# Behind its last product TensorE makes 315 more on consumed buffers, with shifted and strided operands

## The reference

```python
def second_block(x, c, ...):
    c_act = jax.nn.silu(c)
    for l in range(DEPTH_2):
        ...
        x = x + g1 * token_mix(h, w_in[l], w_fourier[l], w_ret[l], w_out[l])
        h = rmsnorm_2(x, norm2_g[l]) * (1.0 + sc2) + sh2
        x = x + g2 * conv_ffn(h, ffn_up[l], conv_w[l], conv_b[l], ffn_down[l])
    return rmsnorm_2(x, final_g)
```

## Time and profile before

| | |
|---|---|
| device time, median of 2 runs | 2907.27 us |
| the two runs | 2906.2 and 2908.34 us |
| span of the profiled execution, first to last instruction | 2902.9 us |
| device time of the profiled execution itself | not listed apart from the two runs |
| TensorE products, weight loads | 19658 each |
| busy: PE, PEld, DVE, ACT, POOL | 99%, 83%, 54%, 38%, 55% |
| mean granted TensorE clock | 0.999 |

### The profile page before, as it was taken

How to read it: one execution, slowest core, us unless ns; L and a number is a source line. 1 busy time by engine, 2 the same in 40 slices (tenths; PEclk the granted TensorE clock), 3 DMA queues, 4 the chain that set the end, 5 groups by cost and what they waited for, 6 DMA issues and landing times.

```text
span 2902.9 us, 49417 instructions
## 1 busy us (share of the span) xinstructions
PE 2885.3 (99%) x19658; PEld 2415.3 (83%) x19658; DVE 1570.4 (54%) x2227; ACT 1109.4 (38%) x1689; POOL 1585.3 (55%) x1912
## 2 busy tenths in 40 slices
PE   9999999999999999999999999999999999999998
PEld 7877777788888888888888898888898888988887
DVE  5467888424556666775434274435763441473635
ACT  4454445333443332443433243333433342342323
POOL 6432233355546666577544556565584444565654
PEclk9999999999999999999999999999999999999999
DMA  4211111233326687433222223232333222232232
GB/s 173 95 46 42 43 55 54 98 138 102 125 85 226 234 280 261 165 124 123 86 87 72 94 88 111 90 106 87 111 126 109 79 89 84 88 102 95 95 102 73
DMA packets 92292, 322.21 MB, mean 111 GB/s; under 512 B 10144, under 2 KB 14368, under 8 KB 91808
## 3 DMA queue, kind: packets, MB, share of 16 engines
q1 hardware_dynamic: 84544, 302.39, 31.6%
q10 hardware_dynamic: 7520, 16.67, 1.7%
HBM read 315.09 MB, written 3.93 MB: 110 GB/s over the span
## 4 chain that ended last, share of the span: by engine, by line
PE 98%; issue 1%; POOL 1%; DVE 1%; DMA 0%; ACT 0%; POOLq 0%; SPq 0%; ACTq 0%; DVEq 0%
PE bank L906 25%; PE bank L910 25%; PE bank L907 25%; PE bank L1254 2%; PE bank L899 2%; PE bank L901 2%; PE bank L900 2%; PE bank L1265 2%; PE bank L1273 1%; PE bank L934 1%; PE bank L936 1%; PE bank L935 1%; PE bank L958 1%; PE bank L960 1%; PE bank L1786 1%
## 5 line engine op out<-in xcount | busy, mean ns | idle before, releaser
L837 POOL TENSOR_TENSOR w_lo<-w_raw,w_hi 128x256 fp32r<-128x256 f32 x1736 | 1420.4, 853 | 984.7 <-ACT w_hi L1863 974.0
L906 PE MATMUL bank<-act,w_hi 128*128 128x512 f32 (+1 forms) x3464 | 1312.1, 379 | 4.2 <-POOL w_lo L837 1.9
L910 PE MATMUL bank<-act,w_lo 128*128 128x512 f32 (+1 forms) x3464 | 1292.0, 373 | 0.0
L907 PE MATMUL bank<-act,w_hi 128*128 128x512 f32 (+1 forms) x3464 | 1290.9, 373 | 0.0
L906 PEld LDWEIGHTS bank<-act,w_hi 128*128 128x128 f32 x3464 | 652.4, 188 | 127.0 <-issue 8.9
L910 PEld LDWEIGHTS bank<-act,w_lo 128*128 128x128 f32 x3464 | 652.2, 188 | 115.5
L907 PEld LDWEIGHTS bank<-act,w_hi 128*128 128x128 f32 x3464 | 652.9, 188 | 106.2
L1863 ACT CAST w_hi<-w_raw 128x1024 fp32r<-128x1024 f32 (+1 forms) x438 | 454.1, 1043 | 338.0 <-DMA w_raw<-in_weights 156.2
L1871 ACT ACTIVATE arena<-bank 128x512 f32<-128x512 f32 (+1 forms) x177 | 104.1, 592 | 416.9 <-PE bank L910 400.3
L855 POOL TENSOR_TENSOR stats<-stats,exponent 128x8 f32<-128x8 f32 (+2 forms) x38 | 46.6, 1226 | 296.6 <-DVE stats L2918 150.2
L2604 DVE TENSOR_TENSOR act<-tmp,act 128x512 fp32r<-128x512 f32 (+1 forms) x140 | 122.2, 873 | 77.2 <-ACT act L1890 72.7
(11 more groups left out here) (362 smaller groups left out, 3067.7 us busy)
## 6 DMA issues: line engine op xcount, KB each, us to landing
w_raw<-in_weights SPq DMA_DIRECT2D x471, 512.0 KB, 3.5
arena<-in_ada SPq DMA_DIRECT2D x96, 512.0 KB, 4.7
arena<-in_strips ACTq DMA_DIRECT2D x8, 448.0 KB, 3.6
arena<-in_x ACTq DMA_DIRECT2D x1, 2048.0 KB, 11.0
y_scratch<-tmp ACTq DMA_DIRECT2D x7, 256.0 KB, 2.0
arena<-y_scratch ACTq DMA_DIRECT2D x1, 1792.0 KB, 7.9
arena<-in_dft ACTq DMA_DIRECT2D x2, 777.5 KB, 4.3
arena<-in_x SPq DMA_DIRECT2D x3, 512.0 KB, 7.3
```

What stands on the lines that cost most here:

```text
L837: ins = nc.gpsimd.tensor_tensor(w_lo[:, k, cols], weights_of(u)[:, cols], w_hi[:, k, cols].bitcast(F32), ALU.subtract)
L906: nc.tensor.matmul(o, wh, xh, start=first, stop=False)
L907: nc.tensor.matmul(o, wh, xl, start=False, stop=False)
L910: mm = nc.tensor.matmul(o, wl, xh, start=False, stop=last)
```

## The change

In TensorE's list, right behind the two transposes at L1823 and the signal `spread_again`, stand 315 products into bank 5. None waits for a semaphore and none signals one; nobody reads bank 5 afterwards. Their operands are `w_hi`, `w_lo` and `acts["A1"]`, which no engine writes by then.

The list `PROBED` has 29 pairs (a, b). For each, nine products of 512 columns are made (three times high-high, high-low, low-high), the moving operand shifted by `a` elements and the weights by `b`: 261 products. Then 18 have weights taken at every second and every fourth element, 9 have a moving operand of two runs of 256 columns from the high and the low half, and 27 have 496, 448 and 128 columns, nine each. 261 + 18 + 9 + 27 = 315. Of these, 288 have 512 columns.

```diff
+PROBED = [(a, 0) for a in (0, 1, 2, 3, 4, 5, 6, 7, 8, 10, 12, 14)] + [(0, b) for b in (1, 2, 4, 8, 12)]
+PROBED += [(4, 4), (8, 8), (3, 3), (8, 4), (4, 8), (12, 4)]
+PROBED += [(16, 0), (32, 0), (64, 0), (0, 16), (0, 32), (0, 64)]
...
             mm.then_inc(sem("spread_again"), 1)
 
+            words = acts["A1"][:].rearrange("p q k s -> p (q k s)")
+            high, low = (x[:].rearrange("p r u -> p (r u)") for x in (w_hi, w_lo))
+            for a, b in PROBED:
+                for k in range(3):
+                    at, wt = S * k + a, P * k + b
+                    x, y = words[:, at:at + S], words[:, KT * S + at:KT * S + at + S]
+                    nc.tensor.matmul(banks[5][:], high[:, wt:wt + P], x, start=k == 0, stop=False)
+                    nc.tensor.matmul(banks[5][:], high[:, wt:wt + P], y, start=False, stop=False)
+                    nc.tensor.matmul(banks[5][:], low[:, wt:wt + P], x, start=False, stop=k == 2)
+            for step in (2, 4):
+                for k in range(3):
+                    x, y = words[:, S * k:S * (k + 1)], words[:, S * (KT + k):S * (KT + k + 1)]
+                    nc.tensor.matmul(banks[5][:], high[:, k:k + step * P:step], x, start=k == 0, stop=False)
+                    nc.tensor.matmul(banks[5][:], high[:, k:k + step * P:step], y, start=False, stop=False)
+                    nc.tensor.matmul(banks[5][:], low[:, k:k + step * P:step], x, start=False, stop=k == 2)
+            pairs = words.rearrange("p (q k s) -> p q k s", q=2, s=S)
+            for k in range(9):
+                x = pairs[:, :, k % 3, 0:W2]
+                nc.tensor.matmul(banks[5][:].rearrange("p (a b) -> p a b", b=W2), high[:, P * k:P * (k + 1)], x,
+                                 start=k == 0, stop=k == 8)
+            for n in (496, 448, 128):
+                for k in range(9):
+                    nc.tensor.matmul(banks[5][:, 0:n], high[:, P * k:P * (k + 1)], words[:, S * k:S * k + n],
+                                     start=k == 0, stop=k == 8)
```

## The result

The changed kernel takes 2972.3 us (two runs, 2972.22 and 2972.37) against 2907.27 before (2906.2 and 2908.34): a ratio of 1.0226, with a 95% interval of 1.0197 to 1.0256. The forecast was 2971 with a range of 2966 to 2978. The size is right to 1.1 us. The span alone came out 3.3 us longer than forecast, and what lies outside the span 2.3 us shorter, so a part of that agreement is luck: two errors against each other.

What follows compares the result with a forecast made beforehand. TensorE bounds the kernel (PE busy 99%), and its list becomes the end: 2896.54 + 65.3 + 4.8, adjusted for the last product, gives a span of 2966.8 us; plus 4.4 outside it, 2971.2 us, range 2966 to 2978.

Steps and rivals of the forecast that it cites:

- The place and the cover: Behind TensorE's last transposes: the stores leave 6.2 us of cover; everything over that is added to the end.
- The narrow products and the unshifted distance: Added block: 288 products of 512 columns at 0.2267 us each, 65.3 us; 27 narrower ones, 4.8 us.
- What shifted starts cost: Added products with shifted operands: no change taken, bounded between -3.8 and +1.9 us over 288 products.
- the row of the retention head: Profile row taken as dear end: 18 distances of 512 columns, 0.2333 us each, 6.6 ns over the tiles.
- the Fourier row: Fourier stage's profile row: odd start, 0.118 us per distance against 0.120 aligned, so an odd start is not dearer.
- All three rivals about addresses and bare products: Added products: addresses lift 13 ns, 2967.4 us (chance 0.09); off-boundary starts halve rate, 2992 (0.05); bare products closer, 2955.8 (0.03).
- the fourth: Rival: added products left out at build, or device time closes with the stores; 2907 us, chance 0.02.
- The clock: At the added block: full work from 2896.5 keeps clock 1.00, no cost; a fall would lose 2.7 us, kept in range.
- A clock of 0.50 within the block: Sign in the added block's profile that would show the forecast wrong; the granted clock was expected at 1.00.
- whatever the shift: Sign expected in the added block: starts of 512-column products lie 0.227 apart at every shift.
- What strided weights cost: 18 added products with weights at every second or fourth element: nothing taken; 2.0 us for step 4 kept in range.
- The outside of the span: Device time beyond the profiled span: 4.4 us added, as in the kernel before, one microsecond to either side.

Runs made afterwards that it cites:

- the kernel with strided weights: Changed kernel with its 315 products replaced by 27 of 512 columns, then groups of twelve at 128 and 256 columns with strided weights and shifted starts: 2956.01 us.

## Why the prediction was right, and where it was not

*The place and the cover* were right: TensorE's list became the end, the stores went on beneath it, and 18 products alone are free.

*The narrow products and the unshifted distance* were right: 0.2267, 0.220 for 496 columns, 0.203 in place of 0.200 for 448, and 4.65 us in place of 4.69 for the 26 distances of the last 27.

*"What shifted starts cost"* took no change between -3.8 and +1.9 us. It is +1.3 (+1.46 with the strided weights), near the dear end. I had given the choice to the row nearest in kind, the tiles, but these have no shift at all; the row of the retention head, 0.2333, was the one that showed operands at other places, and the Fourier row misled. Why its odd start costs nothing stays open. It isn't the 256 columns alone: the last groups of the kernel with strided weights have 256 columns and moving operands shifted by 1, 2 and 4, and in the trace they show 0.121, 0.126 and 0.1165. All three rivals about addresses and bare products fell: no group was under 0.2267, and none near 0.43 once the clock was back. So did the fourth, that the change wouldn't show.

*"The clock"* was costed at nothing with 2.7 in reserve; it took 1.6 us in some executions of the changed kernel and nothing in others. The step of the reasoning that failed is that full work from 2896.5 on would keep the clock: in the profiled execution it fell just then. A clock of 0.50 within the block was named as a sign of being wrong, and in that execution it came. The equal distance "whatever the shift" was named as what would be seen, and it wasn't.

*"What strided weights cost"* was right within 0.12 us, though not wholly for the reason given. The load at step 4 is the one "twice as slow" that "would just hide": it takes 0.233 from load to load, a little over the 0.2267 that hides it. Beside fewer columns the whole of it shows.

*The outside of the span* was the mis-sized term: 4.4 us in the sum, about 2.1 in the runs. It made up for about two thirds of what the shifts, the clock and the 0.3 us at the block's two ends added. That the total came within 1.1 us is therefore luck in part; with 2.1 us outside it the forecast would have been 2968.9, still in its range.

## What to carry to other kernels

Work behind the last product on an engine is free only as long as the stores need; here that was 6.2 us (18 products used 4.2 of them at no cost, and the sum of the longer blocks comes out with 6.2), and each product beyond it cost its full distance of starts, the same as in the middle of the kernel. Take a product's price from the distance of starts of the same type, and start operands of F32R products where the tiles do. Take what lies outside the span from an execution whose span and time are both known.

## What the runs showed that I had not expected

Shifting the starts of F32R operands by a few elements costs up to 11 ns of 227 per product. F32R has 13 ns per product over streaming at 256 and 512 columns, bfloat16 2.5. The clock also fell in the kernel with strided weights while TensorE had products without a gap. Ahead of the fall it made products of 128 columns, from 2904.3 on 0.112 us apart and from 2911.0 on, at step 3, 0.173 apart; at step 4 the clock was at half. The products of 256 columns began at 2929.2, and the clock came back at 2933.8:

```profile
2900.00:2913.00 13.00, 13.00 (x92) 12.24 (x90) 0.00 (x0) 0.00 (x0) 0.00 (x0) 1.00 0.16 53
2913.00:2933.50 20.50, 20.50 (x94) 20.50 (x94) 0.00 (x0) 0.00 (x0) 0.00 (x0) 0.51 0.00 1
2934.00:2953.00 19.00, 19.00 (x121) 19.00 (x120) 0.00 (x0) 0.00 (x0) 0.00 (x0) 1.00 0.00 1
```

The busy column of PE is full in all three stretches (13.00 of 13.00, 20.50 of 20.50, 19.00 of 19.00); only the granted clock tells them apart.
